# Moving two 32-byte spacers in SBUF so that the down weights and the FFN products change sides of a 64-byte boundary

## What is computed

```
for l in range(2):                                   # first block
    h = h + 0.5 * swiglu(rmsnorm(h), wg, wu, wd)     # 1024 -> 2816 -> 1024
    h = h + (pool_mixer | mla_attention)(rmsnorm(h))
    h = h + 0.5 * swiglu(rmsnorm(h), wg, wu, wd)
for l in range(2):                                   # second block
    h = h + 0.5 * rms_norm(swiglu_2(rms_norm(h)))
    h = h + rms_norm((even_mixer | odd_mixer)(rms_norm(h)))
    h = h + 0.5 * rms_norm(swiglu_2(rms_norm(h)))

def swiglu(u, wg, wu, wd):
    return (silu(u @ wg) * (u @ wu)) @ wd
```

## The kernel before, in words

| tensors, in order | start (bytes) | side |
|---|---|---|
| rawA, rawB, hiA, loA, hiB, loB | 16512 (hiA0 41088, hiB0 73856) | even |
| h, xs | 90240, 98432 | even |
| half_line | 106624 | |
| xh, xl | 106656, 114848 | odd |
| act_s, act_h, act_hh, act_hl | 123040 to 129184 | odd |
| row_gain, cols, ident, ident_r, mask_r, ms | 131232 to 141984 | odd |
| ms_eps, rstd, minus_half, flag, act_warm | 142400, 142624, 142848, 142880, 142912 | even, odd, even, odd, even |
| half_line_2 | 142976 | |
| ckvh, ckvl, k_rope, cqh, cql | 143008 to 149152 | odd |
| oh2, ol2, arena | 151200, 159392, 167584 | odd |

## Time and profile before

### The profile page before, as it was taken

One profiled execution on the slowest core, in us unless ns is written; L12 is line 12 of the kernel. 1 busy time (PEld: TensorE's weight loads), 2 busy tenths in 40 slices (PEclk: granted clock), 3 DMA queues, 4 the chain that ended last, 5 costly groups with the idle time before them and its releaser, 6 DMA issues.

```text
span 1996.4 us, 33785 instructions
## 1 busy us (share of the span) xinstructions
PE 1928.9 (97%) x13276; PEld 1771.9 (89%) x13276; DVE 1232.1 (62%) x1651; ACT 943.8 (47%) x1290; POOL 61.7 (3%) x98
## 2 busy tenths in 40 slices
PE   7999999999998989999999998999999999989998
PEld 7999899989997878999899997899989998868997
DVE  5666665565555636656655688666666665767555
ACT  5444544454445535444544457544454446445443
POOL 0000100000000000000100000100000000020000
PEclk9999999999999999999999999999999999999999
DMA  7555355445552125545554433554545553425552
GB/s 263 185 190 193 134 198 189 179 165 199 185 194 100 64 88 198 195 185 188 190 190 187 167 122 122 192 191 188 189 169 190 188 192 116 144 105 182 189 189 95
DMA packets 61119, 338.94 MB, mean 170 GB/s; under 512 B 6816, under 2 KB 7200, under 8 KB 32640
## 3 DMA queue, kind: packets, MB, share of 16 engines
q1 hardware_dynamic: 59040, 330.00, 44.6%
q0 software_dynamic: 2016, 8.06, 1.1%
HBM read 336.98 MB, written 1.05 MB: 169 GB/s over the span
## 4 chain that ended last, share of the span: by engine, by line
PE 87%; DVE 7%; ACT 4%; issue 1%; DMA 1%; POOL 0%; SPq 0%; DVEq 0%; ACTq 0%
PE X L1431 54%; PE Y L1431 32%; DVE arena L1253 2%; DVE loA L958 1%; ACT hiA L528 1%; DVE xl L985 1%; DMA rawA<-in_wa 1%; ACT xh L559 0%; PE Y L1782 0%; POOL rstd L433 0%; DVE h L1018 0%; ACT arena L689 0%; DVE xs L1011 0%; PE X L1465 0%; PE X L1463 0%
## 5 line engine op out<-in xcount | busy, mean ns | idle before, releaser
L1431 PE MATMUL X<-xh,hiA 128*128 128x256 f32 x2592 | 728.9, 281 | 5.8 <-DVE xl L985 5.4
L1431 PE MATMUL X<-xl,hiA 128*128 128x256 f32 x2592 | 725.6, 280 | 0.0
L1431 PE MATMUL X<-xh,loA 128*128 128x256 f32 x2592 | 724.7, 280 | 0.0
L958 DVE TENSOR_TENSOR loA<-rawA,hiA 128x2048 fp32r<-128x2048 f32 x221 | 506.4, 2291 | 296.2 <-ACT hiA L528 296.2
L1431 PEld LDWEIGHTS X<-xh,hiA 128*128 128x128 f32 x2592 | 489.3, 189 | 15.2 <-issue 3.9
L1431 PEld LDWEIGHTS X<-xl,hiA 128*128 128x128 f32 x2592 | 489.1, 189 | 6.6
L1431 PEld LDWEIGHTS X<-xh,loA 128*128 128x128 f32 x2592 | 489.0, 189 | 0.0
L528 ACT ACTIVATE hiA<-rawA 128x2048 fp32r<-128x2048 f32 (+1 forms) x233 | 424.4, 1822 | 82.4 <-PE Y L1431 49.1
L1431 PE MATMUL Y<-hiB,act_hh 128*128 128x512 f32 x704 | 279.4, 397 | 2.6 <-DVE act_hl L1071 2.6
L1431 PE MATMUL Y<-loB,act_hh 128*128 128x512 f32 x704 | 279.2, 397 | 0.0
L1431 PE MATMUL Y<-hiB,act_hl 128*128 128x512 f32 x704 | 279.1, 396 | 0.0
(11 more groups left out here) (234 smaller groups left out, 2072.4 us busy)
## 6 DMA issues: line engine op xcount, KB each, us to landing
rawA<-in_wa SPq DMA_DIRECT2D x221, 1024.0 KB, 5.5
rawB<-in_wb SPq DMA_DIRECT2D x181, 512.0 KB, 3.5
row_gain<-in_rows POOLq DMA_DIRECT2D x8, 512.0 KB, 7.5
arena<-in_gla POOLq DMA_DIRECT2D x1, 1280.0 KB, 10.3
h<-in_x SPq DMA_DIRECT2D x2, 512.0 KB, 4.2
rawA<-in_wa SPq DMA_DIRECT2D x2, 512.0 KB, 6.7
out<-h SPq DMA_DIRECT2D x2, 512.0 KB, 2.7
arena<-in_pool POOLq DMA_DIRECT2D x1, 768.0 KB, 8.5
```

What stands on the lines that cost most here:

```text
L958: nc.vector.tensor_tensor(loA[p][:, :], rawA[p][:, :], hiA[p][:, :].bitcast(f32), ALU.subtract).then_inc(a_lo, 1)
L1431: return say(nc.tensor.matmul(*args, **kw))
```

## The change

The two spacers are allocated earlier: `half_line` between `loA` and `hiB`, `half_line_2` between `xl` and `act_s`. No instruction, size, wait, queue or order changes; only start addresses do.

```
         rawB = [sb(f"rawB{i}", [P, 1024]) for i in range(2)]
         hiA = [sb(f"hiA{i}", [P, 2048], f32r) for i in range(2)]
         loA = [sb(f"loA{i}", [P, 2048], f32r) for i in range(2)]
+        half_line = sb("half_line", [P, 8])
         hiB = [sb(f"hiB{i}", [P, 1024], f32r) for i in range(2)]
         loB = [sb(f"loB{i}", [P, 1024], f32r) for i in range(2)]

         h = sb("h", [P, TT, D])
         xs = sb("xs", [P, TT, D])
-        half_line = sb("half_line", [P, 8])
         xh = sb("xh", [P, KD, TOKENS], f32r)
         xl = sb("xl", [P, KD, TOKENS], f32r)
+        half_line_2 = sb("half_line_2", [P, 8])
         act_s = sb("act_s", [P, 2, TOKENS])
...
         act_warm = sb("act_warm", [P, 16])
-        half_line_2 = sb("half_line_2", [P, 8])
         ckvh = sb("ckvh", [P, TOKENS], f32r)
```

## The result

The changed kernel takes 2006.88 us (median of 5, 2002.15 to 2007.3) against 1995.08 us (median of 5, 1993.03 to 1998.55): ratio 1.0049, 95% interval 1.0038 to 1.0061. It is slower by some 10 us (the ratio compares the means; the medians are 11.8 us apart), outside the predicted range (1988.8 to 1998.8). The profiled execution took 2003.12 us with a span of 2001.2 us.

A forecast was written before the change was run, and what follows sets the result against it. The prediction took TensorE's matmul pace to bound the kernel. All its terms were 0, put on the median of the runs, 1994.05 − 0 = 1994.0 us, with a range of 1988.8 to 1998.8 us.

The forecast's parts named there:

- What bounds the kernel: Whole kernel: TensorE has matmuls under way for 97% of the span and sets the FFNs' pace, covering other engines and transfers.
- Down matmuls: FFN down blocks, 2112 matmuls: swapped operand sides already exist in gate/up at the same pace; 0, bounds −7.0 and +3.2 us.
- Gate/up matmuls: FFN gate/up blocks: their operands keep their addresses, so 0.
- Matmuls on one side: 72 MLA matmuls and the transforms of h, both operands newly on one 64-byte side: 0, at most 0.2 us gained.
- VectorE and ScalarE: Engine instructions on moved tensors: widest gap between sides 8 ns, covered by matmuls; 0, bound ±1.4 us.
- Transfers: Loads to moved places and the store of h: 0, bound +3.3 us for the uncovered store.
- Faster rival: Down blocks lose the 9.4% excess per column, 215 ns a matmul: −38.7 us, 1955.4 us; chance 0.10.
- Slower rival: Down blocks: odd moving operand costs one more 64-byte fetch per matmul, +15.4 us, 2009.5 us; chance 0.08.
- What would make it wrong: FFN matmuls: down's pace depending on side, hiB/loB writes disturbing TensorE's reads, or gate/up leaving 5.60 us per 48.

The follow-up runs named there:

- c_shift32: Kernel before with one more 32-byte spacer ahead of hiA, so hiA and all behind it move up 32 bytes together: 1996.92 us, ratio 1.0004.
- d_stop_after: Changed kernel with four fp32 transposes of ident ahead of each gate/up block but the first two of an FFN: 2067.13 us, ratio 1.0359 to before.
- d_stop_before: Kernel before with four fp32 transposes of ident ahead of each gate/up block but the first two of an FFN: 2077.14 us, ratio 1.0409.
- b_spacer1: Kernel before with only half_line moved ahead of hiB, so hiB, loB, h and xs go up 32 bytes: 1991.07 us, ratio 0.9970.
- a_rest: Kernel before with spacers ahead of h, act_s, act_hh, row_gain; hiB, loB, act_hh, act_hl keep their 64-byte side, oh2 also moved: 2000.11 us, ratio 1.0030.
- d_down64: Kernel before with down's four operands 64 bytes up modulo 128, gate/up's unmoved modulo 128 in seven FFNs: 2007.40 us, ratio 1.0060.
- a_moving_odd: Kernel before with spacers ahead of hiB, h, xh, ckvh; hiB, loB change 64-byte side, act_hh, act_hl don't, xh moves 64 bytes: 2023.38 us, ratio 1.0141.
- a_pair_only: Kernel before with six spacers; hiB, loB, act_hh, act_hl change 64-byte side, xh moves 64 bytes: 2022.49 us, ratio 1.0139.
- c_xh_even: Kernel before with xh, xl 32 bytes lower, all else in place: 2016.98 us, ratio 1.0103.
- c_kick_before: Kernel before with one extra 64-column matmul ahead of each gate/up block but the first two of an FFN: 2018.01 us, ratio 1.0111.
- c_kick_after: Changed kernel with one extra 64-column matmul ahead of each gate/up block but the first two of an FFN: 2021.42 us, ratio 1.0128 to before.

## Why the prediction was wrong

- *What bounds the kernel*: right. TensorE's pace sets the time, all of the shown difference is in it.
- *Down matmuls, 0, bounds −7.0 and +3.2 us*: measured −1.9, inside. The reason given, that the pairing of sides carries over from gate/up, was no reason all the same: c_shift32 exchanges the sides with no effect on either block. That the term came near was luck.
- *Gate/up matmuls, "keep their addresses: 0"*: the step that failed. It measured +9.3 us. I took a block's pace as a function of its own operands. The runs showed that a block settles into one of several rhythms, 116.7 or 117.9 ns here at identical addresses, and that what TensorE did just before it decides which: it switches inside a block at the four fp32 matmuls of the roots, and d_stop_after and d_stop_before exchange the two by four such put ahead. The trace of before had the evidence: its GLA block of the same 48 matmuls, same tensors, took 5.65 us, and by_latent 117.4 ns at the same distance mod 128. I used 117.4 as a bound for down alone. On gate/up, 7680 matmuls × 0.7 ns, or × 1.04 ns by the GLA block, it would have been a bound of +5.4 or +8.0 us and, combined as the others were, a range up to 2001 or 2003: a warning, if still short of 2006.88.
- *Matmuls on one side*: 0. The transforms of h with xs, both odd now, keep their 0.43 us for two (starts at 206.62 and 207.05 us). Of the 72 MLA matmuls, the steps among hiB's with ckvh are 0.12 us in either trace; more about them wasn't measured.
- *VectorE and ScalarE*: 0. Two rows were read for more than they show. The arena row with everything odd (1218 ns) is a product (L1390, ALU.mult), not a subtraction, so no row of before had a subtraction with everything odd; and the update at 748 ns isn't all even, its rstd is odd. The runs show the sides directly, by form: loB takes 1219 ns with hiB, loB even (before) and odd (the changed kernel, b_spacer1), the subtraction of act_hl 426 ns with act_h, act_hh, act_hl odd (before) and even (the changed kernel), the update of h by rstd 748 ns with h, xs even and odd, the one by row_gain 748 ns before and after. ScalarE's hiB takes 1046 ns before and 1049 after, with 1045 to 1053 in a_rest, c_shift32 and d_down64, its act_hh 420 and 419. The 8 ns of the bound showed in none of these VectorE groups.
- *Transfers*: the store kept its 2.7 us; the load of h landed later, 5.1 in place of 4.2 us, but 4.4 in b_spacer1 with h at the same place, so that isn't the side either.
- *Faster rival (no excess left)*: 232.3 ns, not 215; the excess over 213.3 ns, half of the 426.7 that 512 columns take at a granted clock of 0.50, stayed in every placement (229.6 ns in b_spacer1 at the least). The profile gives the clock as a share of full speed only, 0.50 from 12.71 to 15.06 and from 718.93 to 721.70 us. The 2.4 and 1.2 GHz are an estimate from the earlier trace rows: 256 columns in 213.6 ns are 1.2 columns per ns, which is 1.2 GHz if a cycle streams one column, and 2.4 at full speed; that a cycle streams one column isn't shown. The 9.4% needs neither: it is 233.3 against 213.3 ns.
- *Slower rival (one fetch more)*: it had the sign right, but in another block; down got no slower. That a stream is fetched in pieces of 64 bytes was its supposition, and no run shows it: in c_shift32 gate/up streams from an even place and down from an odd one, and they stay at 116.67 and 233.33 ns.
- *What would make it wrong*: "gate/up must stand at 5.60 in any case; if it doesn't, the pace hangs on something else than the addresses of the two operands" is what happened. The chance of 0.08 for slower was too small.

What stays open: what holds the state from one block to the next, why moving down's operands changes the state that down leaves, why a short float32r matmul and another order didn't change the rhythm while four fp32 ones did, and how places map to paces (64 bytes isn't the unit, and equal places mod 128 don't always give equal paces). That gate/up's rhythm depends on what runs ahead of it is shown; why one placement is better than another isn't.

## What to carry to other kernels

Placement in SBUF was worth −0.3% (b_spacer1) to +1.4% (a_moving_odd) to this kernel, which is bound by float32r matmuls, by way of a rhythm that a whole run of matmuls holds (116.7 or 117.9 ns at the same addresses) and that hangs on what ran ahead of it too. These runs give no rule of sides to apply: build the few placements that differ by 32 bytes, run them, and look at the time of a block in the chain, where 5.60 and 5.66 us are plain to see while the mean durations of the page's matmul rows hardly tell (X<-xh,hiA: 281 ns before, 283 after). A tensor that "doesn't move" can't be costed at nothing while what runs just ahead of it moves (here +9.3 us); if one trace shows the same instructions at two paces, the difference is a bound for all of them.

## What the runs showed that I had not expected

- One and the same sequence of 48 matmuls, same operands and places, runs at 116.7 or 117.9 ns per matmul for a whole stage, with a period of four or of three starts; it can switch inside a block at four fp32 matmuls.
- Placement moves gate/up between 116.6 and 120.0 ns (32 bytes of xh: +2.5% of gate/up, 1.0% of the kernel), and down between 229.6 and 234.5. At the lower clock it doesn't show: the first gate/up matmuls take 213 to 214 ns for 256 columns in the changed kernel (12.44 to 17.77 us), a_pair_only and c_xh_even as in the earlier trace rows.
- Behind a matmul of only 64 columns, or four fp32 transposes, the next block's first step takes some 200 ns in place of 117 (198 and 201 in c_kick_before and c_kick_after, 204 and 203 in d_stop_before and d_stop_after). In the rows the weight load of the block's second matmul starts some 80 ns behind its first (81 in the c_kick runs, 83 in the d_stop runs), where in the rest of the block a load starts some 3 ns behind the matmul ahead of it.
